# The tail of a hybrid encoder layer: the order of the last sums, who adds and scales, and the last tile written in halves

## The chip, the core and the metric

The kernel runs on one core of a Trainium2 chip. The metric is the device time of one execution in microseconds, as the median of several timed executions. Before the change it is 700.23 us (three executions, 696.6 to 701.04 us).

## The reference, cut to what matters

One layer of a streaming encoder is applied to 256 frames of a prompt and to 8 streams of 16 frames, so to 384 rows of 1,024 channels. A state-space branch and a retention branch are merged into `x`. Then each row goes through two of 32 experts, and a final norm follows:

```python
x = x + gt2[:, None, :] * hmoe(n2, ...)     # two experts' outputs, weighted, are summed per row
...
y = x * lax.rsqrt(jnp.mean(x * x, axis=-1, keepdims=True) + EPS) * g      # final RMSNorm, g = final_norm
```

Everything in this document is about these last two lines: the sum of the experts' rows, the gate `gt2`, the residual sum, and the final norm.

## The kernel before, in words

The 384 rows stand in T = 3 tiles of 128 rows (0 and 1 the prompt, 2 the streams), each of D = 1,024 channels. The 32 experts are worked through in 16 pairs. For a pair, rows are gathered from DRAM, TensorE multiplies them by the up weights (`up`, L885) and the down weights (`down`, L915), ScalarE scales the result by the routing weight (`rows_out`, L1384), and GpSimd scatters the rows to the DRAM tensor `expert_rows` (`y_d`), which has two places for each token. Weights stream in from DRAM for the whole of this stage.

The last pair is not scattered. Its rows stay in SBUF in `rows2`, written by ScalarE in two halves of 512 columns, and are brought to their tokens by a product with a one-hot matrix, `lastoh[t]`. So the sum of a tile of tokens is made on TensorE in one PSUM bank for each half of its columns: two products with the identity, of the two places of `expert_rows` (`ys[:, t, k]`, L955), and one of `lastoh[t]` with `rows2` (L957). The six sums (three tiles, two halves) are made one after the other in the order of the tiles, in the banks `SUMS`.

All engines run their own programs in the order of the code, with semaphores between them. Around the tail:

- GpSimd waits until all scatters have landed and then signals `rows_out` (L2122). SyncE then issues three loads, one for each tile's `ys` (L1108), each with its own semaphore.
- TensorE makes each sum and signals `y_summed`.
- VectorE waits for a sum, multiplies it from PSUM by the gate `gte` into `ys` (L1916) and adds that to the residual `x2` (L1919). When both halves of a tile are done it signals `x3_ready`.
- ScalarE squares a tile of 1,024 columns and sums its squares (`y3_ssq`, L1420). VectorE turns the sum into a mean (`mean_square`, L1909), GpSimd raises it to the power of -0.5 (L2125), and VectorE multiplies the tile by this number and by the final norm's weights `fnorm` in one instruction (`normed`, L1923).
- ScalarE issues the three writes to `o_y` (L1423), one for a tile, and waits for them.

`x2` and `fnorm` lie in the SBUF tensor that the profile calls working, `ys`, `yout` and `sq3` in the one called weights. `mean_square(t - 1)` stands in VectorE's program between the multiplication and the addition of the second half of tile t, and the first `normed` behind the last addition.

## Time and profile before

| | |
|---|---|
| median of the timed executions | 700.23 us |
| lowest and highest | 696.6 and 701.04 us |
| the profiled execution | 699.47 us |
| its span, first to last instruction | 697.7 us |
| mean granted TensorE clock | 0.987 of full speed |
| busy: TensorE / VectorE / ScalarE / GpSimd | 627.5 / 296.7 / 201.6 / 113.9 us |
| HBM read and written | 183.58 MB and 16.40 MB |

The page names engines PE (TensorE matmuls), PEld (its weight loads), DVE (VectorE), ACT (ScalarE), POOL (GpSimd) and SP (SyncE); a q behind a name is the engine's sequencer. L915 is line 915 of the kernel before. Times of the trace are microseconds from the start of the span. One fp32 product stands as one MATMUL in the program and as two in the trace.

### The profile page before, as it was taken

What the parts mean: (1) busy time and instruction counts of PE and PEld (TensorE: products, weight loads), DVE (VectorE), ACT (ScalarE), POOL (GpSimd) and SP (SyncE); (2) the same over time, 40 slices, a digit from 0 to 9 for tenths busy, and PEclk for the clock granted to TensorE, in tenths of its full rate; (3) what the DMA queues carried; (4) which work ended last, traced back from release to release, by engine and by line L of the source; (5) the groups of instructions that cost most, each with busy time, mean ns of one, the idle gap of its engine ahead of it and who ended that gap; (6) DMA issues with size and microseconds to landing.
All of it is one profiled execution on the core that took longest, in us unless ns stands there. A gap on an engine that the chain in (4) does not pass through costs nothing.

```text
span 697.7 us, 9023 instructions
## 1 busy us (share of the span) xinstructions
PE 627.5 (90%) x3577; PEld 387.2 (56%) x3577; DVE 296.7 (43%) x431; ACT 201.6 (29%) x397; POOL 113.9 (16%) x144
## 2 busy tenths in 40 slices
PE   1789999999999989999999999889999997877883
PEld 0256788877666767667886777533444432322331
DVE  5799896426316567334594737400000000000025
ACT  5478724332334213012003126022122122111111
POOL 6894000010000321001000001202121121121002
PEclk9999999999999999999999999999999999999997
DMA  9942120379655556764454559699999999999962
GB/s 361 432 168 89 49 101 23 121 270 380 242 192 228 205 206 260 281 262 158 154 209 165 208 229 375 246 397 422 418 424 418 420 421 419 423 420 422 365 243 91
DMA packets 30233, 190.42 MB, mean 273 GB/s; under 512 B 5753, under 2 KB 6269, under 8 KB 14960
## 3 DMA queue, kind: packets, MB, share of 16 engines
q1 hardware_dynamic: 20640, 167.50, 60.1%
q0 software_dynamic: 7968, 18.31, 7.2%
q10 hardware_dynamic: 1584, 4.04, 1.5%
q8 instruction: 29, 0.48, 0.3%
q14 instruction: 12, 0.10, 0.0%
HBM read 183.58 MB, written 16.40 MB: 287 GB/s over the span
## 4 chain that ended last, share of the span: by engine, by line
PE 69%; DMA 12%; SPq 8%; DVE 4%; ACT 3%; issue 2%; POOL 1%; POOLq 0%; DVEq 0%; ACTq 0%
PE bank L518 34%; PE bank L885 9%; PE bank L915 5%; DMA working<-in_p_down 5%; DMA weights<-in_p_ada 4%; SPq L1066 3%; SPq L1064 3%; PE bank L497 2%; PE bank L468 2%; DMA working<-in_p_ada 2%; PE bank L617 2%; PE bank L955 2%; SPq L1058 2%; PE bank L527 1%; PE bank L605 1%
## 5 line engine op out<-in xcount | busy, mean ns | idle before, releaser
L518 PE MATMUL bank<-parts,parts 128*128 128x512 f32 x1080 | 259.4, 398 | 3.7 <-DVE working L1674 2.0
L518 PEld LDWEIGHTS bank<-parts,parts 128*128 128x128 f32 x1080 | 200.3, 188 | 63.1 <-issue 14.3
L1878 DVE TENSOR_TENSOR working<-working,bank 128x256 f32<-128x256 f32 x16 | 6.7, 421 | 195.3 <-ACT working L1365 195.3
L885 PE MATMUL bank<-weights,working 128*64 128x512 f32 x352 | 78.5, 594 | 9.0 <-DMA weights<-in_p_up 9.0
L885 PEld LDWEIGHTS bank<-weights,working 128*64 128x64 f32 x352 | 28.5, 137 | 56.9 <-issue 48.5
L1580 DVE TENSOR_TENSOR parts<-weights,parts 128x4096 fp32r<-128x4096 f32 (+1 forms) x10 | 40.0, 3999 | 39.6 <-ACT parts L1178 39.4
L915 PE MATMUL bank<-weights,working 128*64 128x512 f32 x176 | 41.9, 618 | 6.6 <-issue 4.1
L885 PE MATMUL bank<-working 128*64 128x512 f32 x160 | 37.4, 616 | 5.9 <-DMA working<-in_p_up 5.9
L2054 POOL DMA_INDIRECT working<-n_rows,working x15 | 15.3, 1019 | 141.3 <-PE bank L860 118.9
L1384 ACT ACTIVATE working<-bank,working 128x512 f32<-128x512 f32 x32 | 20.4, 684 | 60.9 <-PE bank L915 60.9
L1365 ACT ACTIVATE working<-bank 128x256 f32<-128x256 f32 x16 | 6.2, 385 | 102.8 <-PE bank L885 102.8
L1178 ACT CAST parts<-weights 128x4096 fp32r<-128x4096 f32 x9 | 32.6, 3622 | 5.4 <-DMA weights<-in_p_in 2.9
L885 PEld LDWEIGHTS bank<-working 128*64 128x64 f32 x160 | 13.3, 142 | 29.5 <-issue 24.0
L479 PE MATMUL bank<-weights,working 128*32 128x512 f32 x64 | 12.7, 933 | 18.8 <-DMA weights<-in_p_ada 18.8
L915 PEld LDWEIGHTS bank<-weights,working 128*64 128x64 f32 x176 | 14.2, 141 | 27.2 <-issue 24.1
L1566 DVE TENSOR_TENSOR parts<-weights,parts 128x4096 fp32r<-128x4096 f32 x6 | 26.6, 4426 | 0.2
L617 PE MATMUL bank<-working,weights 128*128 128x384 f32 x64 | 22.7, 517 | 3.2 <-DVE working L1531 3.2
L1258 ACT ACTIVATE working<-bank 128x512 f32<-128x512 f32 x12 | 7.2, 598 | 63.7 <-PE bank L518 63.7
L1565 DVE CAST parts<-weights 128x4096 fp32r<-128x4096 f32 x6 | 13.8, 2294 | 23.2 <-PE bank L518 16.6
L1358 ACT COPY working<-bank 128x512 f32<-128x512 f32 x32 | 17.3, 589 | 18.2 <-PE bank L823 10.8
L2060 POOL DMA_INDIRECT expert_rows<-working x15 | 15.0, 1001 | 45.0 <-ACT working L1384 41.7
L468 PEld LDWEIGHTS bank<-working 128*128 128x128 f32 (+1 forms) x157 | 17.4, 142 | 7.6 <-issue 5.0
(298 smaller groups left out, 729.8 us busy)
## 6 DMA issues: line engine op xcount, KB each, us to landing
weights<-in_p_up SPq DMA_DIRECT2D x21, 2048.0 KB, 21.8
...
```

Source lines behind the costliest of these rows:

```text
L468: ins = nc.tensor.transpose(o[0:n, off:off + m], piece, ident[0:m, 0:m])
L518: ins = mm(o[:, :], x[:, k, 128 * t:128 * t + 128], w[:, k, lo:lo + 512], start=k == 0 and n == 0, stop=k == kt - 1 and n == 2)
L617: ins = mm(o[n][:, 0:NTOK], wv[:, k, 128 * (c + n):128 * (c + n) + 128], nT[:, k, :], start=k == 0, stop=k == KD - 1)
L885: ins = mm(ps[2 + u][64 * e:64 * e + 64, :], xgT[:, u, k, 64 * e:64 * e + 64], ups[slot][:, e, 512 * k:512 * k + 512], start=k == 0, stop= ...
L915: ins = mm(ps[5 + hf][64 * e:64 * e + 64, :], hT[:, u, k, 64 * e:64 * e + 64], downs[slot][e][:, o_:o_ + 512], start=k == 0, stop=k == 1)
L1064: sp.dma_start(downs[2][e], A["p_down"][n, :, e, :]).then_inc(S["down_in2"], 16)
L1066: sp.dma_start(wdown[:, n % 3], A["p_down"][n, :, :, :]).then_inc(S[f"down_in{n % 3}"], 16)
L1178: run(cp(panel_high(key, PANEL, 1), panel(key, PANEL, 1)), "w_high")
L1358: cp(at(B0 + u * 1024 + 512 * c, 512), ps[c][:, :]).then_inc(S["xgT_ready"], 1)
L1384: A_(to[:, 512 * hf:512 * hf + 512], ps[5 + hf][:, :], ACT.Copy, scale=gatecol[:, u, :])\
L1566: run(tt(low, v, high, SUB), ready)
L1580: run(tt(panel_low(key, PANEL, 1)[:, part], panel(key, PANEL, 1)[:, part], panel_high(key, PANEL, 1)[:, part], SUB), "w_split" if hi == PA ...
```

## The change

Only the tail and the names of some semaphores change. The squares' and norms' semaphores of three stages (`x_ssq`, `n2_ssq`, `y3_ssq` and so on) become three shared ones, `row_ssq`, `row_ms` and `row_rstd`, with the counts that they are waited for moved on by what came before. Otherwise:

- **TensorE.** The product of the last pair's rows starts each sum instead of ending it, and five of the six stand ahead of everything that needs `ys`. For tile 0 one identity product, not two, follows.
- **VectorE** adds the two places of tile 0 (`rows_summed`) before anything else. It multiplies all six sums by the gate, but adds only those of tiles 1 and 2 to the residual. It makes the mean of a tile from two half sums. For tile 2 it multiplies the second half by `fnorm` ahead of the mean, and the first half by both behind it.
- **GpSimd** adds tile 0's gated sums to the residual (`x3_first`), multiplies tiles 0 and 1 by `fnorm` (`y_by_norm`), and raises to the power as before.
- **ScalarE** squares each tile in two halves. It multiplies tiles 0 and 1 and the second half of tile 2 by the row's norm (`scaled`).
- **Writes.** SyncE issues those of tiles 0 and 1 and of the first half of tile 2, ScalarE that of its second half.

```diff
@@ -310,7 +310,7 @@
-        sq3 = at(T * D, D)
+        sq3 = at(T * D, 512)
...
@@ -947,14 +947,32 @@
                         down(t, u, slot=u)
             pe.wait_ge(S["records_ready"], 2 + QUARTERS + T)
-            for n, bank in enumerate(SUMS):
-                t, hf = n // 2, n % 2
+            def last_rows(t, hf):
+
+                pe.wait_ge(S["y_copied"], 2 * PAIRS - 1 + hf)
+                mm(ps[SUMS[2 * t + hf]][:, :], lastoh[t], rows2[:, 512 * hf:512 * hf + 512], start=True, stop=False)
+
+            def other_rows(t, hf):
+
                 half = slice(512 * hf, 512 * hf + 512)
-                pe.wait_ge(S[f"ys_in{t}"], 16)
-                for k in range(2):
-                    mm(ps[bank][:, :], ident, ys[:, t, k, half], start=k == 0, stop=False)
-                pe.wait_ge(S["y_copied"], 2 * PAIRS - 1 + hf)
-                mm(ps[bank][:, :], lastoh[t], rows2[:, half], start=False, stop=True).then_inc(S["y_summed"], 1)
+                if t == 0:
+                    pe.wait_ge(S["rows_summed"], 1)
+                else:
+                    pe.wait_ge(S[f"ys_in{t}"], 16)
+                for k in range(1 if t == 0 else 2):
+                    ins = mm(ps[SUMS[2 * t + hf]][:, :], ident, ys[:, t, k, half], start=False, stop=t == 0 or k == 1)
+                ins.then_inc(S["y_summed"], 1)
+
+            for t in range(T):
+                last_rows(t, 0)
+            last_rows(0, 1)
+            last_rows(1, 1)
+            other_rows(0, 0)
+            other_rows(0, 1)
+            last_rows(2, 1)
+            for t in range(1, T):
+                for hf in range(2):
+                    other_rows(t, hf)
         @block.sync
...
@@ -1106,6 +1124,11 @@
             sp.wait_ge(S["rows_out"], 1)
             for t in range(T):
                 sp.dma_start(ys[:, t], y_d.rearrange("(k t p) d -> t p k d", k=2, t=T)[t]).then_inc(S[f"ys_in{t}"], 16)
+            for t in range(T - 1):
+                sp.wait_ge(S["yout_ready"], t + 1)
+                sp.dma_start(A["o_y"][t, :, :], yout[:, t, :]).then_inc(S["hf_out"], 16)
+            sp.wait_ge(S["last_half"], 1)
+            sp.dma_start(A["o_y"][T - 1, :, 0:512], yout[:, T - 1, 0:512]).then_inc(S["hf_out"], 16)
         @block.scalar
...
@@ -1757,12 +1801,12 @@
-                dve.wait_ge(S["n2_ssq"], T + TILES.index(t) + 1)
-                run(stt(stat[:, 32 + t:33 + t], stat[:, 24 + t:25 + t], EPS, stat[:, 36 + t:37 + t], ADD, ADD), "n2_ms")
+                dve.wait_ge(S["row_ssq"], 2 * T + TILES.index(t) + 1)
+                run(stt(stat[:, 32 + t:33 + t], stat[:, 24 + t:25 + t], EPS, stat[:, 36 + t:37 + t], ADD, ADD), "row_ms")
...
@@ -1415,13 +1438,34 @@
                         rows_copy(t, u)
                         silu(t, u)
                         rows_out(t, u)
-            for t in range(T):
-                act.wait_ge(S["x3_ready"], t + 1)
-                run(A_(sq3, x2[:, t, :], ACT.Square, accum_out=stat[:, 40 + t:41 + t]), "y3_ssq")
-            for t in range(T):
-                act.wait_ge(S["yout_ready"], t + 1)
-                act.dma_start(A["o_y"][t, :, :], yout[:, t, :]).then_inc(S["hf_out"], 16)
-            act.wait_ge(S["hf_out"], 16 * (T + 1))
+            def squares3(t, hf):
+
+                if t == 0:
+                    act.wait_ge(S["x3_first"], hf + 1)
+                else:
+                    act.wait_ge(S["x3_ready"], 2 * (t - 1) + hf + 1)
+                col = (40, 20)[hf] + t
+                run(A_(sq3, x2[:, t, 512 * hf:512 * hf + 512], ACT.Square, scale=1.0 / 32.0, accum_out=stat[:, col:col + 1]), "row_ssq")
+
+            def scaled(t, lo, hi):
+
+                act.wait_ge(S["row_rstd"], 1 + T + t + 1)
+                if t == T - 1:
+                    act.wait_ge(S["last_by_norm"], 1)
+                else:
+                    act.wait_ge(S["y_by_norm"], t + 1)
+                run(A_(yout[:, t, lo:hi], yout[:, t, lo:hi], ACT.Copy, scale=stat[:, 57 + t:58 + t]), "yout_ready")
+
+            for t in range(2):
+                for hf in range(2):
+                    squares3(t, hf)
+            scaled(0, 0, D)
+            for hf in range(2):
+                squares3(2, hf)
+            scaled(1, 0, D)
+            scaled(2, 512, D)
+            act.dma_start(A["o_y"][T - 1, :, 512:D], yout[:, T - 1, 512:D]).then_inc(S["hf_out"], 16)
+            act.wait_ge(S["hf_out"], 16 * (T + 2))
         @block.vector
...
@@ -1904,28 +1948,35 @@
                 for hf in range(2):
                     copied(dve, ("g2", v, hf))
             dve.wait_ge(S["tables_in"], 64)
+            def gated(t, hf):
+
+                n = 2 * t + hf
+                half = slice(512 * hf, 512 * hf + 512)
+                y = ys[:, t, 1 if t == 0 else 0, half]
+                dve.wait_ge(S["y_summed"], n + 1)
+                run(tt(y, ps[SUMS[n]][:, :], gte[:, t // 2, half], MUL), "y_gated" if t == 0 else None)
+                if t:
+                    run(tt(x2[:, t, half], x2[:, t, half], y, ADD), "x3_ready")
+
             def mean_square(t):
-                dve.wait_ge(S["y3_ssq"], t + 1)
-                run(ts(stat[:, 44 + t:45 + t], stat[:, 40 + t:41 + t], 1.0 / D, EPS, MUL, ADD), "y3_ms")
-
-            for n, bank in enumerate(SUMS):
-                t, hf = n // 2, n % 2
-                half = slice(512 * hf, 512 * hf + 512)
-                dve.wait_ge(S["y_summed"], n + 1)
-                y = ys[:, t, 0, half]
-                run(tt(y, ps[bank][:, :], gte[:, t // 2, half], MUL))
-                if hf and t:
-                    mean_square(t - 1)
-                run(tt(x2[:, t, half], x2[:, t, half], y, ADD), "x3_ready" if hf else None)
-
-            def normed(t):
-                dve.wait_ge(S["y3_rstd"], t + 1)
-                run(stt(yout[:, t, :], x2[:, t, :], stat[:, 57 + t:58 + t], fnorm, MUL, MUL), "yout_ready")
-
-            normed(0)
-            mean_square(T - 1)
-            for t in range(1, T):
-                normed(t)
+
+                dve.wait_ge(S["row_ssq"], 3 * T + 2 * t + 2)
+                run(stt(stat[:, 44 + t:45 + t], stat[:, 40 + t:41 + t], EPS, stat[:, 20 + t:21 + t], ADD, ADD), "row_ms")
+
+            dve.wait_ge(S["ys_in0"], 16)
+            run(tt(ys[:, 0, 0, :], ys[:, 0, 0, :], ys[:, 0, 1, :], ADD), "rows_summed")
+            gated(0, 0)
+            gated(0, 1)
+            gated(1, 0)
+            gated(1, 1)
+            mean_square(0)
+            gated(2, 0)
+            mean_square(1)
+            gated(2, 1)
+            run(tt(yout[:, 2, 512:D], x2[:, 2, 512:D], fnorm[:, 512:D], MUL), "last_by_norm")
+            mean_square(2)
+            dve.wait_ge(S["row_rstd"], 1 + T + T)
+            run(stt(yout[:, 2, 0:512], x2[:, 2, 0:512], stat[:, 59:60], fnorm[:, 0:512], MUL, MUL), "last_half")
         @block.gpsimd
...
@@ -2120,9 +2171,27 @@
                 pool.wait_ge(S[f"scattered{u}"], 16 * (PAIRS // 2))
             pool.wait_ge(S["cleared"], 16 * (QUARTERS - 1))
             run(nc.gpsimd.memset(gidx, 0), "rows_out")
-            for t in range(T):
-                pool.wait_ge(S["y3_ms"], t + 1)
-                run(tt(stat[:, 57 + t:58 + t], stat[:, 44 + t:45 + t], half[:, 0:1], ALU.pow), "y3_rstd")
+            pool.wait_ge(S["tables_in"], 64)
+
+            def rms(t):
+
+                pool.wait_ge(S["row_ms"], 1 + T + t + 1)
+                run(tt(stat[:, 57 + t:58 + t], stat[:, 44 + t:45 + t], half[:, 0:1], ALU.pow), "row_rstd")
+
+            def by_norm(t):
+
+                run(tt(yout[:, t, :], x2[:, t, :], fnorm, MUL), "y_by_norm")
+
+            for hf in range(2):
+                cols = slice(512 * hf, 512 * hf + 512)
+                pool.wait_ge(S["y_gated"], hf + 1)
+                run(tt(x2[:, 0, cols], x2[:, 0, cols], ys[:, 0, 1, cols], ADD), "x3_first")
+            by_norm(0)
+            rms(0)
+            pool.wait_ge(S["x3_ready"], 2)
+            by_norm(1)
+            rms(1)
+            rms(2)
 # ---- launch: one core ----
```

TensorE's program in order, behind the last pair's down products (L915), of the kernel before. L955 is the identity product, L957 the one of the last pair's rows:

```order
L915 MATMUL bank<-weights,working 64x512 x8
L942 ISA
L942 COMPARE_AND_BRANCH
L935 UNCONDITIONAL_BRANCH
L955 MATMUL bank<-weights,working 128x512 x2
L957 MATMUL bank<-working 128x512
```

The last two rows stand there six times. Of the changed kernel, at the same place, with L953 for the last pair's rows and L963 for the identity product:

```order
L915 MATMUL bank<-weights,working 64x512 x8
L942 ISA
L942 COMPARE_AND_BRANCH
L935 UNCONDITIONAL_BRANCH
L953 MATMUL bank<-working 128x512 x5
L963 MATMUL bank<-weights,working 128x512 x2
L953 MATMUL bank<-working 128x512
L963 MATMUL bank<-weights,working 128x512 x8
L105 UNCONDITIONAL_BRANCH
```

Five products of the last pair's rows have moved in front, and 18 products have become 16.

VectorE's end in the kernel before, from the multiplication (L1916) of tile 2's first half on, with L1919 the addition, L1909 the mean and L1923 the final norm:

```order
L1916 TENSOR_TENSOR weights<-bank,working 128x512
L1919 TENSOR_TENSOR working<-working,weights 128x512
L1916 TENSOR_TENSOR weights<-bank,working 128x512
L1909 TENSOR_SCALAR working<-working 128x1
L1919 TENSOR_TENSOR working<-working,weights 128x512
L1923 SCALAR_TENSOR_TENSOR weights<-working 128x1024
L1909 TENSOR_SCALAR working<-working 128x1
L1923 SCALAR_TENSOR_TENSOR weights<-working 128x1024 x2
```

The whole of VectorE's tail in the changed kernel, with L1967 the addition of tile 0's places, L1957 the multiplication by the gate, L1959 the addition, L1964 the mean, L1976 and L1979 the two halves of tile 2's norm:

```order
L1967 TENSOR_TENSOR weights<-weights 128x1024
L1957 TENSOR_TENSOR weights<-bank,working 128x512 x3
L1959 TENSOR_TENSOR working<-working,weights 128x512
L1957 TENSOR_TENSOR weights<-bank,working 128x512
L1959 TENSOR_TENSOR working<-working,weights 128x512
L1964 SCALAR_TENSOR_TENSOR working<-working 128x1
L1957 TENSOR_TENSOR weights<-bank,working 128x512
L1959 TENSOR_TENSOR working<-working,weights 128x512
L1964 SCALAR_TENSOR_TENSOR working<-working 128x1
L1957 TENSOR_TENSOR weights<-bank,working 128x512
L1959 TENSOR_TENSOR working<-working,weights 128x512
L1976 TENSOR_TENSOR weights<-working 128x512
```

Behind it stand the last mean and L1979. Three instructions of 1,024 columns have left VectorE's end, one has come in front of it, and two of 512 columns stand at its end.

GpSimd's tail, from its last branch on, before:

```order
L2118 REGISTER_ALU
L2111 UNCONDITIONAL_BRANCH
L2122 MEMSET working 128x2
L2125 TENSOR_TENSOR working<-working 128x1 x3
L105 UNCONDITIONAL_BRANCH
```

and now, with L2188 the additions of tile 0, L2183 the multiplications by `fnorm` and L2179 the powers:

```order
L2169 REGISTER_ALU
L2162 UNCONDITIONAL_BRANCH
L2173 MEMSET working 128x2
L2188 TENSOR_TENSOR working<-working,weights 128x512 x2
L2183 TENSOR_TENSOR weights<-working 128x1024
L2179 TENSOR_TENSOR working<-working 128x1
L2183 TENSOR_TENSOR weights<-working 128x1024
L2179 TENSOR_TENSOR working<-working 128x1 x2
L105 UNCONDITIONAL_BRANCH
```

Four wide operations have come between the small ones: the power of tile 0 stands behind three of them, that of tiles 1 and 2 behind all four.

## Rows read from the trace of the kernel before

**Rows 1.** The chain that ended last, 655 to 698: start, us, what.

```profile
657.42 6.15 DMA expert_rows<-working
...
663.74 7.46 DMA weights<-expert_rows
```

**Rows 2.** Timeline, 655 to 698: start us, us, engine line op out<-in xcount [idle before <-releaser].

```profile
665.67 3.67 PE L915 MATMUL bank<-weights,working 128*64 128x512 f32 x16 [0.56 <-issue]
...
669.39 0.69 ACT L1384 ACTIVATE working<-bank,working 128x512 f32<-128x512 f32 x1 [1.05 <-PE bank L915]
...
671.33 1.95 PE L955 MATMUL bank<-weights,working 128*128 128x512 f32 x4 [1.99 <-DMA weights<-expert_rows]
...
686.00 1.02 PE L957 MATMUL bank<-working 128*128 128x512 f32 x2
...
687.13 0.69 DVE L1916 TENSOR_TENSOR weights<-bank,working 128x512 f32<-128x512 f32 x1 [1.16 <-PE bank L957]
...
688.04 0.69 DVE L1919 TENSOR_TENSOR working<-working,weights 128x512 f32<-128x512 f32 x1
...
688.82 1.06 ACT L1420 ACTIVATE weights<-working 128x1024 f32<-128x1024 f32 x1 [4.00 <-DVE working L1919]
...
690.09 0.15 DVE L1909 TENSOR_SCALAR working<-working 128x1 f32<-128x1 f32 x1
...
690.38 1.58 POOL L2125 TENSOR_TENSOR working<-working 128x1 f32<-128x1 f32 x1 [1.25 <-DVE working L1909]
692.07 1.29 DVE L1923 SCALAR_TENSOR_TENSOR weights<-working 128x1024 f32<-128x1024 f32 x1 [0.51 <-POOL working L2125]
```

**Rows 3.** Line L935, the branch of PE behind the last pair: duration ns, start.

```profile
L935 PEldq COMPARE_BRANCH  x1: 365/365/365, 668.3 to 668.3; - x1
```

**Rows 4.** Line L1108, the loads of the expert rows, with times to landing.

```profile
L1108 SPq DMA_DIRECT2D weights<-expert_rows x3: 397/468/469, 663.7 to 664.7; - x3
...
DMA to landing us min/median/max: 7.5/9.5/11.5
```

**Rows 5.** Groups of POOL by form: busy us, mean ns | idle before us.

```profile
L1986 POOL TENSOR_TENSOR working<-working 128x512 f32<-128x512 f32 x4 | 8.7, 2170 | 0.3
...
L2035 POOL TENSOR_TENSOR working<-working 128x1 f32<-128x1 f32 x3 | 1.7, 557 | 96.0 <-DVE working L1761 96.0
...
L1965 POOL TENSOR_TENSOR working<-working 128x512 f32<-128x512 f32 x1 | 1.0, 1040 | 0.1
...
L1965 POOL TENSOR_TENSOR working<-working 128x256 f32<-128x256 f32 x1 | 0.6, 614 | 0.1
```

**Rows 6.** Timeline of DVE, 36 to 39.4, beside operations of POOL.

```profile
36.36 0.69 DVE L1530 TENSOR_TENSOR working<-bank,working 128x512 f32<-128x512 f32 x1
37.09 0.82 DVE L1531 TENSOR_TENSOR working<-working 128x512 f32<-128x512 f32 x1
...
39.39 2.17 DVE L1536 TENSOR_TENSOR weights<-weights 64x1024 f32<-64x1024 f32 x1
```

**Rows 7.** Groups of ACT by form: busy us, mean ns | idle before us.

```profile
L1301 ACT ACTIVATE working<-working 128x512 f32<-128x512 f32 x6 | 3.8, 633 | 26.3 <-DVE working L1756 26.2
...
L1147 ACT ACTIVATE working<-working 128x1024 f32<-128x1024 f32 x3 | 3.4, 1148 | 0.1
...
L1306 ACT ACTIVATE working<-working 128x512 f32<-128x512 f32 x3 | 2.2, 726 | 1.5 <-POOL working L2035 1.1 <-ACT working L1324 0.4
...
L1301 ACT ACTIVATION_READ_ACCUMULATOR working<-working 128x1 f32 x6 | 1.1, 187 | 0.0
```

**Rows 8.** Group of DVE by form, the addition of 1,024 columns.

```profile
L1511 DVE TENSOR_TENSOR weights<-working 128x1024 f32<-128x1024 f32 x4 | 5.0, 1246 | 0.1
```

**Rows 9.** Line L1423, the writes of the output, with times to landing.

```profile
L1423 ACTq DMA_DIRECT2D out_o_y<-weights x3: 338/338/343, 690.1 to 693.4; - x3
...
DMA to landing us min/median/max: 2.6/2.7/2.7
```

**Rows 10.** Window during the output writes: us, busy by engine, PEclk, DMA share, GB/s.

```profile
691.00:692.00 1.00, 0.00 (x0) 0.00 (x0) 0.56 (x1) 0.00 (x0) 0.96 (x1) 0.50 1.00 406
```

30 lines of the change are left out of this document (15 added, 15 removed).

## The prediction, made before the changed kernel ran

> **What bounds the kernel now.** I read the chain of waits first, then the timeline of its last 30 us. The chain ends in the tail: the last scatter lands 6.15 us after its issue, and the first load of `ys` 7.46 us after its own, at 671.20 [rows 1]. TensorE had been free since 669.34 (665.67 + 3.67) and begins the sums at 671.33, released by that load. From there it works without a gap to 687.02 (686.00 + 1.02) [rows 2]. Its 36 instructions, two for each of 18 products, start every 0.43 us ((686.00 - 671.33) / 34), so a product costs 0.86 us, and what a row shows of an instruction (1.02 for two) reaches 0.16 us past the start of the next. Behind TensorE comes a string of single steps, each waiting for the one before: gate 687.13, addition 688.04, square 688.82, mean 690.09, power 690.38, norm 692.07 to 693.36 [rows 2]. The last write is issued at 693.4 and lands 2.64 us later, at 696.0 [rows 9]. From there to the span's end at 697.7, 1.7 us, and from the span to the execution's 699.47, nothing changes. So any time that the last write lands earlier counts in full, and there are two places to gain: 15.7 us of TensorE with a start that waited, and 9.0 us from its end to the last landing.
>
> **TensorE.** Two products are gone: 1.72 us. The five that need only `rows2` can start as soon as the down products end: by the overlap above the next may start at 669.34 - 0.16 = 669.18. ScalarE has the first half of `rows2` ready before, and the second at 670.08 (669.39 + 0.69) [rows 2], in time for the fourth product at 671.76. The sequencer has done its branch at 668.7 [rows 3]. So the start moves by 671.33 - 669.18 = 2.15 us. The 32 instructions start every 0.43 us and end at 669.18 + 13.76 + 0.16 = 683.10 instead of 687.02, 3.9 us earlier. Is anything late? Tile 0's sum needs VectorE's addition, 1,024 columns at 1.25 us [rows 8], from 671.3 to 672.55; its product's turn comes at 669.18 + 4.30 = 673.48, so the addition costs nothing, with 0.9 us of cover. If the load came more than 0.9 us later, each further tenth would be paid. The loads of tiles 1 and 2, issued at 664.2 and 664.7, land after 9.5 and 11.5 us, at 673.7 and 676.2 [rows 4]; their turns come at 676.06 and 679.5. The six sums are then complete at 674.50, 675.36, 677.94, 679.66, 681.38 and 683.10.
>
> **GpSimd's price.** No row of the tail shows a wide operation there. An addition of 512 columns took 1.04 us where VectorE let it, and 2.17 beside VectorE's long ones; 256 columns took 0.61 [rows 5]. By the step from 256 to 512 (0.43), 1,024 columns take 1.04 + 0.86 = 1.90 us. I take 1.04 and 1.90, since VectorE is mostly idle or reading PSUM here, and keep 2.17 as the other bound.
> The Trainium skill's GPSIMD Engine Reference ("Elementwise — side-by-side cycle accounting") gives 4,497 ns for 2,048 columns, an estimate of 2.25 us for 1,024; the sum by it would come out some 0.35 us worse than mine. The trace's 1.04 us at 512 columns is a little below it.
>
> **The two engines together.** A VectorE operation with one input in PSUM ran in 0.69 us beside GpSimd, the next, with both inputs in SBUF, in 0.82, and one of 1,024 columns in 2.17 us, against about 1.25 for 1,024 columns at another place [rows 6, 8]. The other way round, a power took 1.58 us beside VectorE's norm and 0.557 alone [rows 2, 5]. I read this as one of the two being held until the other ends. So an addition to `x2` is held by a running GpSimd operation, a gate multiplication isn't.
> The Trainium skill says the same and more strictly, in SBUF — State Buffer ("SBUF: two separate sides"): the shared pair of ports is locked for a whole instruction, the loser waits. It speaks against this change, which puts two 1.90 us operations beside additions; the trace agrees with it.
>
> **The steps**, with 0.1 us from one engine to another and 0.03 within one. Gates of tile 0 on VectorE 674.6 to 675.3 and 675.5 to 676.2. GpSimd adds 675.4 to 676.45 and 676.5 to 677.6, then multiplies tile 0 by `fnorm` to 679.5. Tile 1: gate 678.05 to 678.75, its addition is held to 679.5 and ends 680.2; gate to 680.9, addition to 681.6. Mean of tile 0 by 681.8. GpSimd's power, 0.557 us [rows 5], to 682.45, and at 682.5 it wants its second 1.90 us. At the same 682.5 VectorE, with tile 2's first gate done, wants its addition. I cannot tell from rows who is first; I take VectorE, since an operation of GpSimd touches its data somewhat after its row begins. Then: addition to 683.2, mean of tile 1 to 683.4, the last gate (sum at 683.10) to 684.1. Now the last addition is held by GpSimd's operation, which worked from 683.2 to about 685.0: 684.95 to 685.65. Before, it ended at 688.73: 3.1 us gained so far, of TensorE's 3.9.
> Then ScalarE squares 512 columns in 0.63 + 0.19 us, scales tile 1 in 1.15 us and half of tile 2 in 0.73 us [rows 7], with 0.05 between them: 686.5, 687.7, 688.45. The last mean and power lie beside tile 1's scaling (686.65 and 687.3), VectorE's half is done by 688.0. The last write is issued at 688.5, against 693.4: from the last addition on 2.85 us instead of 4.65.
> The writes: 512 KB at 406 GB/s [rows 10] take 1.29 of their 2.64 us, so 1.35 are fixed. Tile 1 is issued 0.75 us ahead of the last half and tile 2's two halves are another 512 KB: 1.35 + 2 x 1.29 - 0.75 = 3.2 us. Landing 691.7 instead of 696.0. **Gain 4.3 us.** The new names of semaphores cost nothing: each wait is for the same event.
>
> From the profiled execution's own 699.47 that is **695.2 us**. Its time stands 0.8 below the median of 700.23 and near the mean of the three runs (699.3), so I leave it as the forecast of the median.
>
> **The rivals.**
> - GpSimd is first at 682.5. Tile 2's first addition waits to 684.4, the last ends at 686.7, the last write is issued at 689.5: gain 3.3, **696.2 us**. Same rows, the order of a tenth of a microsecond decides.
> - Nobody holds anybody: the gates and additions follow TensorE, the last addition ends at 684.6, the last issue is at 687.4: gain 5.4, **694.1 us**. Against it stand 2.17 and 1.58 us [rows 2, 6].
> - The change's first step does nothing: the five products start no earlier than 671.33, because the instructions behind the branch are not there yet or the last pair ends late against the loads. Two products less remain, all steps lie 2.15 us later: gain 2.15, **697.3 us**. For it speaks only that TensorE did nothing between 668.7 and 671.2 that would show it ready; against it, that it started 0.13 us behind the load.
> - Slower or no faster than before: GpSimd becomes the end. From 675.4 it has two additions of p and two multiplications of 1.82p (1.90 / 1.04), three powers and gaps: done at 677.6 + 5.64p, last write issued 1.3 later. At p = 2.17, its dearest row, that is 691.1 + 3.2 = 694.3, gain 1.7, **697.8 us**. It decides from p = 2.47 (no gain), and at p = 3.7 the kernel is 1% slower, **706.5**. No row has such a price.
>
> **How the numbers follow.** Chances: forecast 0.42, GpSimd first 0.23, nobody held 0.13, no early start 0.10, GpSimd the end without gain 0.05; 0.07 for what I don't see. The mechanisms reach from 694.1 to 697.8. The three runs before differ by 4.4 us for reasons that lie ahead of the tail, so a median of a few may stand 1 to 2.5 us off: range **691.8 to 698.5**. About 1% (7 us) is what a measurement of this kernel can tell from no change. Every likely case gains 2 to 5.4 us, so within 1% is 0.82; faster by more 0.15, for a low median on top of 4 to 5 us; slower by more 0.03.
>
> **What would show it.** TensorE's L953 starts near 669.2 and there are 32 tail instructions ending 3.9 us earlier. VectorE's L1967 ends before L963 starts. L2188 takes about 1.05 us, L2183 about 1.9 (more where VectorE came first). One of tile 1's additions (L1959) is long or late, and one of tile 2's. From the last L1959 to the last write 2.85 us. Wrong would be a start at 671, an L2183 over 3 us, a last power later than ScalarE's scaling of tile 1, or writes that take over 4 us to land.

## The result, and the profile after

The changed kernel takes 697.54 us (median of 20 executions, 695.62 to 701.34), the kernel before, on the same chip, 700.62 us (20 executions, 696.6 to 702.57). The ratio of the two, from all these executions, is 0.9968 with a 95% interval of 0.9953 to 0.9983, so the changed kernel is 2.2 us faster, between 1.2 and 3.3 (the two medians alone are 3.1 us apart). The forecast was 695.2 us, from a gain of 4.3 us in the tail counted from the profiled execution's 699.47. The sign and the range (691.8 to 698.5) held; of the gain, about half is missing. All ratios here leave out three executions far outside the rest: 823.9 and 3,552.92 us of the kernel mean_by_scalar and 1,289.73 us of the kernel before.

From the page of the changed kernel:

```profile
span 699.1 us, 9034 instructions
PE 625.7 (90%) x3573; PEld 386.1 (55%) x3573; DVE 297.1 (43%) x429; ACT 205.3 (29%) x406; POOL 117.3 (17%) x148
PEclk9999999999999999999999999999999999999997
```

The profiled execution of after is 1.4 us longer than that of before (699.1 against 697.7), though the medians stand the other way. The cause lies ahead of the tail: the last down product (L915) ends at 672.84 here and at 669.34 before. From 560 to 670 us TensorE waited 19.1 us for loads of weights here and 17.6 us before; that is part of the 3.5 us, and the rest was not traced. So from here on everything in the tail is measured from the end of the last down product and written with a plus: the span's end is at +28.34 before (697.68 - 669.34) and at +26.28 after (699.12 - 672.84). That is 2.06 us, and it agrees with the 2.2 us of the ratio.

TensorE in the tail, timeline of after (start us, us, engine, line, operation, tiles, count, idle time before it and its releaser):

```profile
669.18 3.65 PE L915 MATMUL bank<-weights,working 128*64 128x512 f32 x16 [0.56 <-issue]
672.77 4.56 PE L953 MATMUL bank<-working 128*128 128x512 f32 x10
677.16 1.88 PE L963 MATMUL bank<-weights,working 128*128 128x512 f32 x4
678.88 1.02 PE L953 MATMUL bank<-working 128*128 128x512 f32 x2
679.74 7.03 PE L963 MATMUL bank<-weights,working 128*128 128x512 f32 x16
```

The pause of 2 us ahead of the sums [rows 2] is gone: L953 starts right behind L915. There are 32 instructions, and they end at 686.77, which is +13.93, where before they ended at +17.68. TensorE gained 3.75 us; 3.9 were forecast.

VectorE, same view:

```profile
681.73 0.69 DVE L1957 TENSOR_TENSOR weights<-bank,working 128x512 f32<-128x512 f32 x1 [1.89 <-PE bank L963]
682.45 2.37 DVE L1959 TENSOR_TENSOR working<-working,weights 128x512 f32<-128x512 f32 x1
684.85 0.69 DVE L1957 TENSOR_TENSOR weights<-bank,working 128x512 f32<-128x512 f32 x1
...
686.50 0.69 DVE L1957 TENSOR_TENSOR weights<-bank,working 128x512 f32<-128x512 f32 x1
687.23 0.69 DVE L1959 TENSOR_TENSOR working<-working,weights 128x512 f32<-128x512 f32 x1
687.95 2.23 DVE L1964 SCALAR_TENSOR_TENSOR working<-working 128x1 f32<-128x1 f32 x1
690.21 0.69 DVE L1957 TENSOR_TENSOR weights<-bank,working 128x512 f32<-128x512 f32 x1
690.94 0.69 DVE L1959 TENSOR_TENSOR working<-working,weights 128x512 f32<-128x512 f32 x1
```

and GpSimd beside it:

```profile
680.50 1.27 POOL L2188 TENSOR_TENSOR working<-working,weights 128x512 f32<-128x512 f32 x1
681.86 2.42 POOL L2183 TENSOR_TENSOR weights<-working 128x1024 f32<-128x1024 f32 x1
686.61 0.56 POOL L2179 TENSOR_TENSOR working<-working 128x1 f32<-128x1 f32 x1 [2.34 <-DVE working L1964]
687.25 2.91 POOL L2183 TENSOR_TENSOR weights<-working 128x1024 f32<-128x1024 f32 x1
```

Two rows on VectorE are long. An addition of 512 columns takes 2.37 us instead of 0.69 and ends 0.55 us behind GpSimd's first multiplication (684.28). And the mean of tile 1 (L1964), an instruction of **one column**, takes 2.23 us and ends with GpSimd's second multiplication (690.16). Behind it stand the last gate and the last addition. TensorE's last sum was complete at 686.77; its gate starts at 690.21. The finished sum waited 3.4 us for VectorE, where before it waited 0.1 (687.02 to 687.13 [rows 2]). The last addition ends at 691.63, which is +18.79; before it ended at 688.73, which is +19.39 [rows 2].

From there to the last write's issue, ScalarE and its queue, same view:

```profile
691.72 0.63 ACT L1448 ACTIVATE weights<-working 128x512 f32<-128x512 f32 x1 [2.57 <-DVE working L1959]
...
692.48 1.90 ACT L1457 ACTIVATE weights<-weights,working 128x1024 f32<-128x1024 f32 x2
694.41 0.35 ACTq L1467 DMA_DIRECT2D out_o_y<-weights  x1
```

That is 2.78 us (694.41 - 691.63), and 4.65 before. The write lands after 3.29 us, 2.64 before [rows 9]. So the last landing gains 0.60 + 1.87 - 0.65 = 1.8 us: +24.86 instead of +26.68. The span gained 2.06, a quarter of a microsecond more, which the landing does not explain; that difference turned out to have a cause of its own (below, "What ends the execution").

### The profile page after: what moved, and what is told of

It reads as the page before. It is cut to its first block, busy times and chain, and to the rows that moved or that the text cites. A ratio compares the mean times of both kernels' runs of the same rounds, so it can differ in the third digit from the quotient of the medians.

```text
span 699.1 us, 9034 instructions
## 1 busy us (share of the span) xinstructions
PE 625.7 (90%) x3573; PEld 386.1 (55%) x3573; DVE 297.1 (43%) x429; ACT 205.3 (29%) x406; POOL 117.3 (17%) x148
## 4 chain that ended last, share of the span: by engine, by line
PE 67%; SPq 12%; DMA 11%; DVE 4%; ACT 3%; issue 2%; POOL 0%; DVEq 0%; ACTq 0%; POOLq 0%
PE bank L518 34%; PE bank L885 9%; DMA weights<-in_p_up 5%; PE bank L915 4%; DMA weights<-in_p_ada 4%; SPq L1084 4%; SPq L1076 3%; SPq L1082 3%; PE bank L497 2%; PE bank L468 2%; DMA working<-in_p_ada 2%; PE bank L617 2%; SPq L1074 2%; PE bank L527 1%; PE bank L605 1%
## 5 line engine op out<-in xcount | busy, mean ns | idle before, releaser
L885 PE MATMUL bank<-weights,working 128*64 128x512 f32 x352 | 81.9, 614 | 12.8 <-DMA weights<-in_p_up 12.8
L915 PE MATMUL bank<-weights,working 128*64 128x512 f32 x176 | 40.2, 597 | 6.6 <-issue 4.9
L885 PE MATMUL bank<-working 128*64 128x512 f32 x160 | 35.8, 594 | 3.9 <-DMA working<-in_p_up 3.9
L915 PEld LDWEIGHTS bank<-weights,working 128*64 128x64 f32 x176 | 13.8, 136 | 25.9 <-issue 23.8
L1609 DVE CAST parts<-weights 128x4096 fp32r<-128x4096 f32 x6 | 13.8, 2294 | 23.2 <-PE bank L518 16.6
```

Source lines behind the costliest of these rows:

```text
L885: ins = mm(ps[2 + u][64 * e:64 * e + 64, :], xgT[:, u, k, 64 * e:64 * e + 64], ups[slot][:, e, 512 * k:512 * k + 512], start=k == 0, stop= ...
L915: ins = mm(ps[5 + hf][64 * e:64 * e + 64, :], hT[:, u, k, 64 * e:64 * e + 64], downs[slot][e][:, o_:o_ + 512], start=k == 0, stop=k == 1)
```

## Experiments

A held instruction is here one that lasts until GpSimd's has ended, although it is short by itself. The theory after the two traces: (A) the missing gain is GpSimd's hold on VectorE's instructions with both inputs in SBUF. Rivals: (B) the new order of the products gives less than TensorE's rows promise; (C) GpSimd is simply slower than forecast and its own chain is the end. The column "tail" is the span's end behind the last down product in the profiled execution; ratios are to the kernel before on the same chip, with 95% intervals.

| kernel | last addition ends | last landing | tail, us | ratio |
|---|---|---|---|---|
| before | +19.39 | +26.68 | 28.34 | |
| after | +18.79 | +24.86 | 26.28 | 0.9968 (0.9953 to 0.9983) |
| order_only | +17.37 | +24.66 | 26.31 | 0.9963 (0.9939 to 0.9987) |
| order_and_sum | +15.64 | +22.91 | 24.59 | 0.9949 (0.9923 to 0.9976) |
| without_order | +19.59 | +25.68 | 27.08 | 0.9982 (0.9960 to 1.0005) |
| mean_by_scalar | +17.94 | +24.02 | 25.48 | 0.9957 (0.9929 to 0.9985) |
| gated_in_psum | +15.46 | +21.93 | 23.01 | 0.9915 (0.9882 to 0.9948) |
| quarters | +16.38 | +24.04 | 25.07 | 0.9959 (0.9940 to 0.9978) |
| two_sums | +14.32 | +21.10 | 22.14 | 0.9908 (0.9877 to 0.9939) |
| shared_norm | +14.32 | +20.43 | 22.49 | 0.9917 (0.9889 to 0.9945) |
| root_on_scalar | +21.22 | +28.49 | 28.90 | 1.0001 (0.9976 to 1.0025) |
| root_on_scalar_again | +19.58 | +26.84 | 27.25 | 0.9987 (0.9964 to 1.0010) |
| gpsimd_early | +14.71 | +20.89 | 21.30 | 0.9907 (0.9881 to 0.9934) |

Many intervals of the ratios overlap; the tails tell more than the ratios do, though each is of one execution. How well a tail repeats is seen in gpsimd_prices (below), which is order_and_sum up to its last write: the last addition ends at +15.64 in both, and the last write lands at +22.93 and +22.92.

### The order of the products alone, then with VectorE's sum of tile 0

order_only is the kernel before with TensorE's new order, three products for each sum as before:

```diff
+            for t in range(T):
+                last_rows(t, 0)
+            last_rows(0, 1)
+            last_rows(1, 1)
+            other_rows(0, 0)
+            other_rows(0, 1)
+            last_rows(2, 1)
...
```

> The kernel before with one part of the change: the last pair's products first, in the changed kernel's order, still 18 products, everything behind TensorE as before. If the early start is real (my step: 2.15 us), TensorE's tail starts at once behind the down products and the whole gain of 2.0 to 2.2 us reaches the last write, ratio 0.997. If the early start is lost to the string of steps behind TensorE, or if the last pair's end and the rows' landing vary against each other from run to run, it gains under 1 us. In the trace: from the end of the last down product to the last landing 24.6 us, against 26.7 before and 24.9 in the changed kernel.

order_and_sum adds VectorE's addition of tile 0's two places, and so one product less for each of its sums:

```diff
+            dve.wait_ge(S["ys_in0"], 16)
+            run(tt(ys[:, 0, 0, :], ys[:, 0, 0, :], ys[:, 0, 1, :], ADD), "rows_summed")
```

> The same with VectorE adding tile 0's places, so 16 products; norm, powers, squares and writes as before. Theory (VectorE is held by GpSimd's wide operations in the changed kernel): with no such operations here, TensorE's whole 3.75 us come through, 22.9 us from the last down product to the last landing, 3.5 to 3.8 us faster than before, ratio 0.9947, and so faster than the changed kernel (24.9 us). Rival (the changed kernel's loss is in TensorE or in the loads): this kernel loses it too and stays near 24.9 us, ratio 0.997.

Measured: the tail is 2.03 us shorter with the order (28.34 to 26.31) and another 1.72 with the sum (to 24.59). The forecast's two terms for TensorE were 2.15 and 1.72. So rival B falls, and more than that: these two edits alone give 3.75 us, all that TensorE gained, while the whole change gives 2.06. **The other parts of the change cost 1.7 us** in the profiled tails, where they were to give 0.4 (4.3 - 3.9). The ratios point the same way (0.9949 against 0.9968) but don't separate the two.

### The rest of the change without the order

```diff
-            dve.wait_ge(S["ys_in0"], 16)
-            run(tt(ys[:, 0, 0, :], ys[:, 0, 0, :], ys[:, 0, 1, :], ADD), "rows_summed")
```

and TensorE's sums as in the kernel before, in the kernel after.

> The changed kernel with TensorE's part undone: the sums as before, 18 products in the old order, no addition of tile 0's places on VectorE. What GpSimd, ScalarE and the writes do is the changed kernel's. The two parts apart: TensorE's gave 3.77 us in order_and_sum, the whole change 1.8. If gains added, this part alone would lose 1.9 us (from the first landing of the expert rows to the last landing of the output 26.7 us against 24.8 before). Theory (VectorE's slack decides what a hold costs; here TensorE brings a sum every 2.58 us, so 1.1 us of each hold is hidden): the last addition comes within 0.3 us of where it was before, the shorter end gains 1.85 and the writes lose 0.65, 23.8 us, ratio 0.9985.

Measured: tail 27.08, 1.26 us better than before (the interval of the ratio reaches 1.0005, so the timed executions can't tell it from no gain). So the same parts that cost 1.7 us behind the early sums give 1.3 us behind the late ones. The holds are there too; both multiplications of GpSimd (2.40 us each) meet an addition of VectorE:

```profile
681.85 1.83 DVE L1941 TENSOR_TENSOR working<-working,weights 128x512 f32<-128x512 f32 x1
...
687.38 1.67 DVE L1941 TENSOR_TENSOR working<-working,weights 128x512 f32<-128x512 f32 x1
```

But a sum comes only every 2.58 us here, so VectorE has pauses that take up the delay, and the last addition ends 0.2 us later than before (+19.59 and +19.39). The parts don't add up, and neither is bad by itself.

### The mean without a second tensor input

mean_by_scalar is after with the half sums added as a per-row scalar, not as a second tensor:

```diff
-                run(stt(stat[:, 44 + t:45 + t], stat[:, 40 + t:41 + t], EPS, stat[:, 20 + t:21 + t], ADD, ADD), "row_ms")
+                run(ts(stat[:, 44 + t:45 + t], stat[:, 40 + t:41 + t], stat[:, 20 + t:21 + t], EPS, ADD, ADD), "row_ms")
```

> The changed kernel; only the mean of a tile is made by an instruction with one tensor input and the second half sum as its scalar, in place of one with two tensor inputs. In the changed kernel's trace tile 1's mean, one column, took 2.226 us beside GpSimd's multiplication. Theory (any VectorE instruction with two SBUF inputs is held, however small): the mean takes 0.16 us, the last gate follows at once, and then the last addition is held instead, until GpSimd's multiplication ends; the gate has moved under the hold, gain over the changed kernel 0.7 to 0.9 us. Rival (the mean waited for ScalarE's square, or any VectorE instruction on SBUF is held): the mean still takes over 2 us and nothing is gained.

VectorE, timeline of mean_by_scalar, tile 1's mean and what follows:

```profile
685.85 0.21 DVE L1964 TENSOR_SCALAR working<-working 128x1 f32<-128x1 f32 x1
686.10 0.69 DVE L1957 TENSOR_TENSOR weights<-bank,working 128x512 f32<-128x512 f32 x1
686.83 1.80 DVE L1959 TENSOR_TENSOR working<-working,weights 128x512 f32<-128x512 f32 x1
```

The mean is no longer held (0.21 us, and 2.23 with two tensors), beside the same GpSimd multiplication (2.92 us from 685.15 on). But the hold goes on to the next instruction with two inputs in SBUF, the last addition (1.80 instead of 0.69). This is the picture that the prediction drew, and the tail gains 0.8 us by it (26.28 to 25.48): 0.7 for the gate, which no longer stands behind the hold, and 0.1.

### No addition with two inputs in SBUF

gated_in_psum is mean_by_scalar with one more edit: for tiles 1 and 2 the gate writes its result back to its PSUM bank, so the addition has one input there:

```diff
-                y = ys[:, t, 1 if t == 0 else 0, half]
+                y = ps[SUMS[n]][:, :] if t else ys[:, t, 1, half]
```

> The same, and the gate multiplication of tiles 1 and 2 writes its product back to its PSUM bank, so that each addition reads one input from PSUM and one from SBUF. Theory (held only with two SBUF inputs): no addition and no mean lasts over 0.8 us, VectorE follows TensorE, its last addition ends about 1.5 us behind TensorE instead of 4.9, and the kernel gains about 3.3 us over the changed one: 21.6 us from the last down product to the last landing, 5 us faster than before, ratio 0.993. Rival (GpSimd's own chain of wide operations and powers sets the end): VectorE is early, but the powers stay where they were, the last one near 20 us behind the last down product, and at most 1 us is gained over the changed kernel.

GpSimd's two multiplications of 1,024 columns in gated_in_psum (line, engine, operation, count: ns min/median/max, first and last start), and VectorE beside the second of them:

```profile
L2183 POOL TENSOR_TENSOR weights<-working x2: 2409/2418/2426, 678.4 to 682.5; 128x1024 f32<-128x1024 f32 x2
```

```profile
682.45 0.69 DVE L1959 TENSOR_TENSOR working<-working,bank 128x512 f32<-128x512 f32 x1
683.17 0.21 DVE L1964 TENSOR_SCALAR working<-working 128x1 f32<-128x1 f32 x1
683.43 0.70 DVE L1957 TENSOR_TENSOR bank<-bank,working 128x512 f32<-128x512 f32 x1
684.16 0.69 DVE L1959 TENSOR_TENSOR working<-working,bank 128x512 f32<-128x512 f32 x1
```

VectorE is held nowhere: all additions take 0.69 us, and GpSimd's multiplications take 2.41 and 2.43. The last addition ends at +15.46, 3.3 us earlier than in after, and the tail is 23.01, 3.3 us shorter. GpSimd still takes 2.4 us for a multiplication, as for the first one in after (2.42; the second took 2.91 there, beside an addition that had begun 0.03 us before it), and its chain did not keep the end at 26. That decides for theory A against C as the cause of what is missing in after, and it is the whole of the missing gain and more. The tail is 5.3 us better than before and the ratio agrees: 0.9915, 5.9 us of 700.3, from 3.6 to 8.3, an interval that doesn't touch that of after.

Against the prediction's rival "nobody held" the last addition is close (+15.46; it had 684.6, so +15.26), but the landing gained 4.75 us, not 5.4. Here GpSimd's chain comes through: its power of tile 1 stands behind its second multiplication, takes 1.05 us instead of 0.56 beside VectorE's multiplication by `fnorm` (both inputs in SBUF) and ends at 685.99; ScalarE stood idle for 0.4 us ahead of its scaling of tile 1, which needs it.

### The hold made shorter

quarters is after with GpSimd's multiplications in pieces of 256 columns:

```diff
-                run(tt(yout[:, t, :], x2[:, t, :], fnorm, MUL), "y_by_norm")
+                for q in range(4):
+                    part = slice(256 * q, 256 * q + 256)
+                    run(tt(yout[:, t, part], x2[:, t, part], fnorm[:, part], MUL), "y_by_norm")
```

> The changed kernel with each of GpSimd's multiplications by the final norm's weights cut into four of 256 columns. Theory (a hold lasts as long as the GpSimd instruction that runs): no VectorE instruction is held for over 0.8 us, where 1.7 and 2.1 us stood; GpSimd itself takes longer in all (4 x 0.8 = 3.2 us instead of 2.4), and the last addition comes 1 to 1.7 us earlier: 23.2 to 23.9 us from the last down product to the last landing, against 24.9. Rival (the two share the memory's ports by turns of a few columns, so the length of an instruction doesn't matter and what counts is how many columns both have): VectorE's additions are slowed as much in sum as before, no gain, or a loss for GpSimd's longer chain, 24.9 us or more.

Measured: the longest held instruction of VectorE lasts 1.10 us, its last addition ends at +16.38, 2.4 us earlier than in after. But the tail is only 1.2 us shorter (25.07), and the last write lands at +24.04, outside the 23.2 to 23.9 that were expected. GpSimd, timeline of quarters:

```profile
681.98 4.44 POOL L2185 TENSOR_TENSOR weights<-working 128x256 f32<-128x256 f32 x4
686.50 1.18 POOL L2179 TENSOR_TENSOR working<-working 128x1 f32<-128x1 f32 x2
```

The four quarters of tile 1 take 4.44 us where one multiplication took 2.91 (those of tile 0 take 3.83 where it took 2.42). Single pieces take 0.73 to 1.26 us, the long ones where a two-input instruction of VectorE had begun before them (the first of tile 1 at 681.98, the addition at 681.95): now GpSimd is held too. Its power of tile 1 comes at 686.50, and ScalarE stands idle for 1.61 us until it is done. The hold was shared out, not removed. In this kernel rival C is true: GpSimd's own chain is the end.

### Two better kernels

two_sums is gated_in_psum with tile 1's two places also added by VectorE (two products less on TensorE). shared_norm is two_sums with half of tile 1's norm multiplication on VectorE instead of GpSimd:

```diff
+            dve.wait_ge(S["row_rstd"], 1 + T + 2)
+            run(stt(yout[:, 1, 512:D], x2[:, 1, 512:D], stat[:, 58:59], fnorm[:, 512:D], MUL, MUL), "vector_half")
...
+                cols = slice(0, (D, 512)[t])
+                run(tt(yout[:, t, cols], x2[:, t, cols], fnorm[:, cols], MUL), "y_by_norm")
```

> From gated_in_psum (21.9 us from the last down product to the last landing): VectorE adds the two places of tile 1 as well, in its idle time behind the addition of tile 0, so TensorE has 14 products. If TensorE's pace still sets the end there, two products less are 1.72 us and most of it arrives: 20.2 to 20.7 us, ratio 0.989. Rival (VectorE or GpSimd is the bound by now): VectorE's last addition follows TensorE's end by more than 1.6 us or GpSimd's powers end the string, and under 0.8 us is gained: 21.1 us or more.

> From two_sums (21.1 us from the last down product to the last landing, GpSimd's power of tile 1 late at 683.9 behind its second multiplication): GpSimd multiplies only the first half of tile 1 by the final norm's weights, ScalarE scales only that half, and VectorE makes the second half in one instruction behind its last addition. If GpSimd's chain set the end of two_sums, the power of tile 1 comes 1.2 us earlier, ScalarE's scaling begins right behind its last square, and the write of tile 1 no longer queues ahead of the last halves: 20.2 to 20.4 us. Rival (the end is set by VectorE's string, which gets 0.75 us more to do): 21 us or more.

Measured: two_sums has a tail of 22.14 us and 0.9908, 692.79 us against 699.72. TensorE ends 1.72 us earlier than in gated_in_psum, but the landing gains only 0.83 us (+21.10): the expectation's rival came true. VectorE's last addition ends 2.1 us behind TensorE's end, and the chain that ends last runs through GpSimd's second multiplication (2.42 us from 680.52 on) and the power behind it. In shared_norm this power ends 1.4 us earlier and the last write lands 0.67 us earlier than in two_sums (+20.43, as expected, and +21.10), **and the span ends 0.35 us later** (22.49, 22.14). A landing that comes earlier and an end that comes later don't fit the prediction's sentence that any time that the last write lands earlier counts in full.

### What ends the execution

gpsimd_prices is order_and_sum with ten more GpSimd operations behind everything else, whose results nobody uses; so that GpSimd could be measured undisturbed (one execution, 714.36 us):

```diff
+            for n in range(2):
+                run(tt(apart[:, 0:512], x2[:, 0, 0:512], fnorm[:, 0:512], MUL))
+                run(tt(apart[:, 0:512], x2[:, 0, 0:512], fnorm[:, 0:512], ADD))
+                run(tt(as_rows(apart[:, 0:512], 32), as_rows(x2[:, 0, 0:512], 32), bc(fnorm[:, 0:16], 2, 32), MUL))
+                run(tt(as_rows(apart[:, 0:512], 32), as_rows(x2[:, 0, :], 64)[:, :, 0:32], as_rows(fnorm, 64)[:, :, 0:32], MUL))
+                run(tt(apart, x2[:, 0, :], fnorm, MUL))
```

> order_and_sum with ten GpSimd operations added behind the end of all VectorE work, which nothing waits for: the disputed price by itself. Twice each: a multiplication and an addition of 512 contiguous columns, a multiplication whose second operand repeats each of 16 values 32 times (the form of the row at 1.04 us that I priced from), one whose operands are pieces of 32 columns with gaps, and a multiplication of 1,024 columns. If the price hangs on the operands' form, the contiguous ones take 1.27 and 2.4 us and the repeated one 1.04. If 1.04 is the undisturbed price and the 1.27 of the tail is a disturbance by VectorE, all of 512 columns take about 1.04 here and 1,024 about 1.9.

Its groups on GpSimd, in the order of the diff (ns min/median/max):

```profile
L2150 POOL TENSOR_TENSOR weights<-working x2: 1262/1263/1264, 691.6 to 699.1; 128x512 f32<-128x512 f32 x2
L2151 POOL TENSOR_TENSOR weights<-working x2: 1261/1262/1262, 692.9 to 700.5; 128x512 f32<-128x512 f32 x2
L2152 POOL TENSOR_TENSOR weights<-working x2: 1047/1047/1047, 694.3 to 701.8; 128x512 f32<-128x512 f32 x2
L2153 POOL TENSOR_TENSOR weights<-working x2: 1254/1254/1254, 695.4 to 703.0; 128x512 f32<-128x512 f32 x2
L2154 POOL TENSOR_TENSOR weights<-working x2: 2339/2340/2341, 696.7 to 704.3; 128x1024 f32<-128x1024 f32 x2
```

So 512 columns cost 1.25 to 1.26 us, added or multiplied, in one run or in pieces. Only the form whose second operand is one value repeated over 32 columns takes 1.05, and the row of 1.04 us that the prediction went by [rows 5] was of that form (L1965).

The same kernel showed something else: the last write had landed at 694.11, GpSimd's last operation ended at 706.62, and the span ended at 712.34. In all eleven traces up to here the span ends 5.71 or 5.72 us behind GpSimd's last operation. Behind it stands line 105, where each engine's program ends; its DRAIN is an instruction of the engine's queue that the profile shows there. In after (columns as above):

```profile
L105 POOLq COMPARE_BRANCH  x1: 38/38/38, 693.4 to 693.4; - x1
L105 POOLq DRAIN  x1: 5297/5297/5297, 693.6 to 693.6; - x1
...
L105 ACTq DRAIN  x1: 8/8/8, 697.9 to 697.9; - x1
```

GpSimd's DRAIN takes 5.297 us, every time, and ScalarE's 0.008. So in after the end is GpSimd's last power (693.40) + 5.72 = 699.12, and the last write, landed at 697.70, did not set it. This doesn't bring rival C back: that power takes 0.55 us and waits for tile 2's mean, which waits for the late last addition. To test this, root_on_scalar leaves GpSimd without work behind the scatters, in the kernel before (the first line of the diff only has ScalarE ready for roots ahead of the tail):

```diff
+            run(A_(stat[:, 63:64], const[:, C_ONE:C_ONE + 1], ACT.Sqrt))
...
-                run(ts(stat[:, 44 + t:45 + t], stat[:, 40 + t:41 + t], 1.0 / D, EPS, MUL, ADD), "y3_ms")
+                run(ts(stat[:, 44 + t:45 + t], stat[:, 40 + t:41 + t], 1.0 / D, EPS, MUL, ADD))
+                run(nc.vector.reciprocal(stat[:, 44 + t:45 + t], stat[:, 44 + t:45 + t]), "y3_ms")
...
+                act.wait_ge(S["y3_ms"], t + 1)
+                run(A_(stat[:, 57 + t:58 + t], stat[:, 44 + t:45 + t], ACT.Sqrt), "y3_rstd")
...
-            for t in range(T):
-                pool.wait_ge(S["y3_ms"], t + 1)
-                run(tt(stat[:, 57 + t:58 + t], stat[:, 44 + t:45 + t], half[:, 0:1], ALU.pow), "y3_rstd")
```

> The kernel before, with one thing changed: the last stage's power -0.5 of a row's mean is made as a reciprocal on VectorE and a square root on ScalarE, so GpSimd does nothing at all behind the scatters (its last operation is 30 us ahead of the end). Theory (GpSimd's last operation plus 5.72 us sets the end of an execution, not the last write): that bound is gone, the span ends less than 1.4 us behind the landing of the last write (before: 1.66 us), and from the last down product to the span's end are 26.0 to 27.0 us in place of 28.34: about 1.0 us from the shorter string of steps (a power took 1.58 us beside VectorE's norm, a root and a reciprocal together about 0.5), the rest from the end. Ratio near 0.997. Rival (the last write sets the end, and a fixed 1.4 to 1.7 us follow it): the last write lands about 1.0 us earlier and the span ends 1.66 us behind it as before, so the span gains just what the landing gains.

> The same kernel as root_on_scalar, once more. In its profiled execution TensorE's granted clock stood at 0.69 of full speed from 670 to 675 us, behind a pause of 1.9 us in which it waited for the load of ys, and the sums took 1.5 us longer; in the profile of the kernel before the same pause was followed by full speed. If that fall was chance, this profile has the sums at full speed, from the last down product to the span's end are about 27.4 us (28.90 less 1.54; before 28.34), 0.41 us behind the last landing, and the ratio is near 0.998. If the kernel brings it about, the fall is there again, the stretch is 28.9 us again and the ratio stays at 1.000.

The last write of root_on_scalar_again, issue and landing, and its line 105:

```profile
L1426 ACTq DMA_DIRECT2D out_o_y<-weights x3: 338/338/343, 692.3 to 694.6; - x3
...
DMA to landing us min/median/max: 2.7/2.9/3.0
```

```profile
L105 POOLq DRAIN  x1: 5297/5297/5297, 665.4 to 665.4; - x1
...
L105 ACTq COMPARE_BRANCH  x1: 38/38/38, 697.5 to 697.5; - x1
```

The drain is now over 27 us ahead of the end, the last write lands at 697.49, and the span ends at 697.90: 0.41 us behind the landing, in both runs of it, where before it was 1.66. The step on the end is settled. The rest of the first run's expectation was wrong. Its tail was 28.90 and not 26.0 to 27.0, for a reason told below, and in the second run too the landing did not come 1.0 us earlier (+26.84, before +26.68). The power of 1.58 us [rows 2] lay mostly beside VectorE's norm of tile 1, so from the last addition to the last issue only 0.27 us went (4.65 to 4.38); the reciprocals in VectorE's program put the last addition 0.19 us back (+19.39 to +19.58), and the last write took 2.89 us to land instead of 2.64. So 1.1 us are gained in the tail of the second run, all from the end, and the ratio of 0.9987 (0.9964 to 1.0010) can't tell them from nothing.

In the first of the two runs TensorE was slow in the middle of the tail. Windows of root_on_scalar (stretch, length, busy time of PE, PEld, DVE, ACT, POOL with counts, granted clock, DMA share, GB/s):

```profile
670.00:675.00 5.00, 3.84 (x6) 1.69 (x7) 0.00 (x0) 1.49 (x2) 0.00 (x0) 0.69 0.84 334
```

and of root_on_scalar_again:

```profile
670.00:675.00 5.00, 3.02 (x10) 1.21 (x7) 0.00 (x0) 2.17 (x3) 0.00 (x0) 1.00 0.99 400
```

In the first, behind the pause in which TensorE waited 1.9 us for `ys`, three of its instructions start 0.853 us apart instead of 0.429, and from 672 to 675 us the granted clock is 0.50, so the lower of its two levels, 1.2 GHz instead of 2.4. The sums end 1.6 us late. In the second run, with a pause of 2.0 us, the clock stays at 1.00; so it does in before and in without_order, with pauses of 2.0 us. So neither the program nor the pause brings it about every time. After has no such pause, and whether it is spared this fall now and then is open.

gpsimd_early puts both findings together: shared_norm with the roots on ScalarE, so that GpSimd ends with its second multiplication.

```diff
-                run(ts(stat[:, 44 + t:45 + t], stat[:, 40 + t:41 + t], stat[:, 20 + t:21 + t], EPS, ADD, ADD), "row_ms")
+                run(ts(stat[:, 44 + t:45 + t], stat[:, 40 + t:41 + t], stat[:, 20 + t:21 + t], EPS, ADD, ADD))
+                run(nc.vector.reciprocal(stat[:, 44 + t:45 + t], stat[:, 44 + t:45 + t]), "row_ms")
...
+                act.wait_ge(S["row_ms"], 1 + T + t + 1)
+                run(A_(stat[:, 57 + t:58 + t], stat[:, 44 + t:45 + t], ACT.Sqrt), "rooted")
```

> The kernel of shared_norm with the three roots on ScalarE (reciprocal on VectorE), so that GpSimd's last operation is its second multiplication by the final norm's weights. Theory (GpSimd's end plus 5.72 us): its last operation ends about 14.5 us behind the last down product, not 16.8, and so bounds the end at 20.3 us; the last write lands at +19.9 to +20.5 and then sets it, with 0.5 to 1.2 us behind it: span's end at +20.5 to +21.5 in place of 22.49 (shared_norm) and 22.14 (two_sums), a further 1 to 2 us, ratio to the kernel before near 0.989. Rival (the last write and a fixed 1.0 to 2.1 us behind it): the end stays at 22.0 or later, ratio 0.991 to 0.992.

```profile
L105 POOLq DRAIN  x1: 5297/5297/5297, 686.3 to 686.3; - x1
```

GpSimd's drain is over at 691.6, the last write lands at 693.94 (+20.89), and the span ends 0.41 us later, at +21.30. That is 1.2 us less than shared_norm though the write lands 0.46 us later, and 7.0 us less than before. The span's end is within the expected +20.5 to +21.5; the write lands later than the expected +20.5 at most, and GpSimd is done at +13.05 instead of +14.5. It is the shortest tail of all, and in the timed executions the kernel takes 693.71 us against 699.34, ratio 0.9907. It can't be told from two_sums (0.9908): the difference of 0.84 us between their tails is smaller than the width of these intervals (0.5% is 3.7 us).

## Why the prediction was right and wrong

The prediction's steps failed where VectorE and GpSimd meet: the last addition came 2.48 us later than forecast, and that is all of what the landing lacks (1.8 us gained instead of 4.3). Two steps made it: GpSimd's operations were priced too low, so that its second multiplication, and the hold with it, ended 1.66 us late; and a held mean was priced as a free one, which cost 0.82 us more.

**TensorE: right.** It starts at once behind the down products (forecast 2.15 us earlier; order_only gained 2.03), and two products less give 1.72 us (as forecast; order_and_sum), together 3.9 forecast and 3.75 found. VectorE's sum of tile 0 (674.79 to 676.02) was done 1.1 us before its product wanted it, as said.

**GpSimd's price: wrong by 0.23 and 0.5 us.** 512 columns took 1.27 instead of 1.04, 1,024 columns 2.42 instead of 1.90. The step that failed is the choice of the row: 1.04 was the cheaper of the two rows of 512 columns [rows 5], and of an operand form that this change doesn't have. (The prediction calls both rows additions; in the kernel L1965 and L1986 are multiplications, which gpsimd_prices shows to cost the same.) The range was held open to 2.17, but the steps were worked with 1.04 and 1.90.

The Trainium skill's GPSIMD Engine Reference ("Elementwise — side-by-side cycle accounting") gave an estimate of 2.25 us for 1,024 columns, which the prediction set aside; the measured 2.34 (alone) and 2.42 are nearer to it. The prediction said that the sum would come out 0.35 us worse by it; but in its own steps both multiplications stand ahead of the last addition, so it would have been 2 x 0.35 = 0.7 us.

**Who holds whom: right in kind, wrong in what it reached.** Tile 1's first addition was held (2.37 us; forecast 1.45, from 678.75 to 680.2), and at the second meeting VectorE's addition was first, by 0.03 us (687.225 and 687.254), as taken. But the prediction gave the means 0.2 us each and held neither, although its own rule was that VectorE's instructions with both inputs in SBUF are held, and the change had just given the mean a second one. The mean of tile 1 took 2.23 us, and it stood ahead of the last gate, so that gate and addition (1.42 us) came behind the hold and not the addition alone.

The Trainium skill's SBUF — State Buffer ("SBUF: two separate sides") has a lock for a whole instruction, which whoever starts first gets. This trace agrees, also for a VectorE instruction of one column, which the prediction had not drawn from it: that one ended 0.02 us behind GpSimd's.

The last addition ended at +18.79 where +16.31 (685.65 - 669.34) was forecast, 2.48 us late. In the rows that is: GpSimd's second multiplication began 1.25 us later than forecast (+14.41 instead of +13.16). Its first addition had started 0.26 us late, its two additions took 0.5 us longer and its first multiplication 0.52, and tile 1's addition, held by it, passed this on. The second multiplication ended another 0.41 us late (+17.32 instead of +15.66), and 0.82 us is the order behind the hold. mean_by_scalar took away the last of these and gained 0.8 us. gated_in_psum took away every hold and gained 3.3, at GpSimd's true prices: without a hold they don't reach VectorE.

**The end string and the writes: right.** 2.78 us from the last addition to the last issue (forecast 2.85), 3.29 us to the landing (forecast 3.2).

**From the landing to the end: wrong, and by luck cheap.** "Nothing changes" behind the last landing was read off one trace, where the difference of 1.66 us looked like a fixed cost. It was the distance of two independent ends: last landing + 0.41, and GpSimd's last operation + 5.72. GpSimd's last power moved from +22.62 to +20.56, 2.06 us, and that is the gain of the span. With the landing it would have been 1.82. The step cost little here, since the forecast's own last power, by 687.3, gives an end at 693.0 instead of 697.7, a gain of 4.7 and not 4.3. That the two ends lay this close is luck. The step would have cost more where the choice was between two_sums and shared_norm.

Of the rivals, none is what happened. The measured 697.54 us lies between those of "no early start" (697.3) and "GpSimd becomes the end" (697.8), but by chance: TensorE did start early, and GpSimd's 1,024 columns took 2.42 us and not the 3.9 (1.82 x 2.17) of the other. That the range held says as little, since the missing gain was inside it by those two rivals. "Nobody held" is nearly what gated_in_psum does. "GpSimd becomes the end" had the right engine but worked with its throughput; its place at the end came from the drain behind its smallest operation.
